# Two blocks of a transformer on one core: the modulation's weighted sum moves from GpSimd to VectorE, its loads from the sync queue to GpSimd's

## The reference

```python
mod = silu(c) @ w_mod[l] + b_mod[l]          # 2048 x 6144: shift, scale, gate
shift, scale, gate = split(mod, 3)
h = rms_norm(x, g_pre[l]) * (1 + scale) + shift
...
x = x + gate * rms_norm(y, g_post[l])
```

## Time and profile before

| | |
|---|---|
| Median of 3 runs | 4131.22 us (4123.99 to 4135.74) |
| Span of the profiled execution, first to last instruction | 4126.4 us |
| Its own time | the page gives no other than the span; the median of the runs is 4.8 us above it |
| TensorE busy | 3789.4 us (92%) |
| VectorE busy | 1773.6 us (43%) |
| ScalarE busy | 1140.1 us (28%) |
| GpSimd busy | 977.8 us (24%) |
| Moved by DMA | 430.07 MB, mean 104 GB/s |

### The profile page before, as it was taken

One profiled execution on the slowest core, in us unless ns is written; L12 is line 12 of the kernel. 1 busy time (PEld: TensorE's weight loads), 2 busy tenths in 40 slices (PEclk: granted clock), 3 DMA queues, 4 the chain that ended last, 5 costly groups with the idle time before them and its releaser, 6 DMA issues.

```text
span 4126.4 us, 54228 instructions
## 1 busy us (share of the span) xinstructions
PE 3789.4 (92%) x17149; PEld 2959.1 (72%) x17149; DVE 1773.6 (43%) x2992; ACT 1140.1 (28%) x1952; POOL 977.8 (24%) x842
## 2 busy tenths in 40 slices
PE   7999898899799988889979999997897999998898
PEld 5777677578677766756868876785686887786586
DVE  3342762542534266253352335346525224534643
ACT  3232151132313114213232224223223223422231
POOL 6746726200475673530000000003000000000300
PEclk9999899999899999999989985898899997599799
DMA  6645415133464552422233320220333321032042
GB/s 228 188 128 161 143 53 175 53 113 105 146 190 124 164 158 64 151 77 92 94 111 93 102 62 1 85 91 1 143 93 112 96 88 41 8 101 66 1 163 102
DMA packets 211419, 430.07 MB, mean 104 GB/s; under 512 B 21206, under 2 KB 28785, under 8 KB 204824
## 3 DMA queue, kind: packets, MB, share of 16 engines
q1 hardware_dynamic: 206952, 402.96, 31.2%
q10 hardware_dynamic: 2928, 21.02, 1.2%
q0 software_dynamic: 1344, 3.76, 0.4%
HBM read 406.58 MB, written 24.75 MB: 105 GB/s over the span
## 4 chain that ended last, share of the span: by engine, by line
PE 75%; POOL 9%; DVE 7%; issue 5%; DMA 2%; ACT 1%; POOLq 0%; DVEq 0%; SPq 0%; ACTq 0%
PE bank L642 17%; PE bank L644 17%; PE bank L643 17%; PE bank L677 7%; PE bank L695 5%; POOL macc L1865 5%; POOL mprod L1858 4%; PE bank L686 3%; PE bank L669 2%; DMA stage<-in_w_in 1%; PE bank L665 1%; PE bank L656 1%; DVE late L1720 1%; PE bank L796 1%; DMA wmod<-in_w_mod 1%
## 5 line engine op out<-in xcount | busy, mean ns | idle before, releaser
L642 PE MATMUL bank<-wlo,act_hi 128*128 128x512 f32 (+1 forms) x3968 | 1571.3, 396 | 100.5 <-DVE wlo L1189 52.0
L643 PE MATMUL bank<-whi,act_hi 128*128 128x512 f32 (+1 forms) x3968 | 1551.7, 391 | 0.0
L644 PE MATMUL bank<-whi,act_lo 128*128 128x512 f32 (+1 forms) x3968 | 1550.0, 391 | 0.0
L1189 DVE TENSOR_TENSOR wlo<-stage,whi 128x1024 fp32r<-128x1024 f32 (+1 forms) x496 | 645.1, 1308 | 1338.7 <-ACT whi L943 1335.3
L943 ACT ACTIVATE whi<-stage 128x1024 fp32r<-128x1024 f32 (+1 forms) x496 | 516.1, 1048 | 1628.1 <-DMA stage<-in_w_in 865.4
L642 PEld LDWEIGHTS bank<-wlo,act_hi 128*128 128x128 f32 x3968 | 755.7, 190 | 285.2 <-DVE wlo L1189 64.7
L644 PEld LDWEIGHTS bank<-whi,act_lo 128*128 128x128 f32 x3968 | 755.6, 190 | 156.4
L643 PEld LDWEIGHTS bank<-whi,act_hi 128*128 128x128 f32 x3968 | 756.9, 191 | 148.3
L1858 POOL TENSOR_SCALAR mprod<-wmod,csil 128x512 f32<-128x512 f32 x384 | 366.8, 955 | 806.7 <-DVE Y L1349 309.0
L1900 POOL TENSOR_TENSOR late<-late 128x512 f32<-128x512 f32 x48 | 66.8, 1403 | 2026.3 <-DVE late L1737 2026.3
L1865 POOL TENSOR_TENSOR macc<-macc,mprod 128x512 f32<-128x512 f32 x360 | 512.4, 1423 | 66.0 <-POOL mprod L1858 66.0
(11 more groups left out here) (198 smaller groups left out, 2516.3 us busy)
## 6 DMA issues: line engine op xcount, KB each, us to landing
stage<-in_w_in SPq DMA_DIRECT2D x352, 512.0 KB, 3.8
wmod<-in_w_mod SPq DMA_DIRECT2D x384, 256.0 KB, 2.9
stage<-in_w_out SPq DMA_DIRECT2D x128, 512.0 KB, 3.7
out<-Y ACTq DMA_DIRECT2D x20, 1024.0 KB, 5.0
zone<-out SPq DMA_DIRECT2D x4, 4096.0 KB, 14.6
stage<-in_w_in SPq DMA_DIRECT2D x16, 320.0 KB, 3.3
Y<-in_x SPq DMA_DIRECT2D x4, 1024.0 KB, 9.1
rpb_tiles<-rpb_pad POOLq DMA_DIRECT2D x16, 224.0 KB, 4.4
```

Source lines behind the costliest of these rows:

```text
L642: pe.matmul(out, hi_x, lo_w, start=(k == 0), stop=False)
L643: pe.matmul(out, hi_x, hi_w, start=False, stop=False)
L644: mm = pe.matmul(out, lo_x, hi_w, start=False, stop=(k == KC - 1))
L1189: dve.tensor_tensor(wlo[:, j % RH, :, 0:width], stage[:, j % RS, :, 0:width], whi[:, j % RH, :, 0:width].bitcast(F32), ALU.subtract).then_ ...
```

## The change

- VectorE takes the sum: a new `mod_pair` does two tiles, each in one instruction macc = wmod * column + macc (the first of a panel is a plain product). A pair follows each of the eight splits of a panel. Before the first tile it waits until TensorE has summed the macc of the panel before.
- The twelve modulation panels no longer lie in the twelve w_in panels. They go with panels 0 to 6, 9 and 10 and with output panels 13, 14 and 15, so that the panels with extra work on VectorE (7, 8, 11) have none.
- GpSimd computes nothing of it. It issues the loads of w_mod (`mod_loads`), each as soon as its buffer is free, from its own queue. It builds the bias tiles first.
- The sync queue loads w_in without modulation loads in between.
- TensorE's row sum comes one panel later, after the first double of that panel, and ScalarE sends the row out in that panel. The last one stands after panel 15.
- The squares of the output panels go to a new buffer junk in place of macc.

```diff
@@ sync @@
-            def mod_double(l, p, j):
-                for k in (2 * j, 2 * j + 1):
-                    sp.wait_ge(mod_used.sem, mod_used.at(0, l, p * KC + k + 1 - 2))
-                    ...
             def in_panel(l, p, col, width=PW):
                 for j in range(ND):
                     double(0, l, p, j, io["w_in"], col, width)
-                    mod_double(l, p, j)
@@ tensor @@
                     if j < ND - 1:
                         mm.then_inc(w_used.sem, 1)
+                    if j == 0 and row is not None:
+                        mod_row_sum(l, row)
...
-                in_panel(l, 0, src=xs)
+                panel(0, l, 0, src=xs)
                 with pe.Fori(1, 4) as p:
-                    in_panel(l, p)
+                    panel(0, l, p, row=p - 1)
...
-                with pe.Fori(4, 9) as p:
-                    in_panel(l, p)
+                with pe.Fori(4, 8) as p:
+                    panel(0, l, p, row=p - 1)
+                panel(0, l, 8)
...
-                in_panel(l, 9)
-                in_panel(l, 10, B_CKV_W)
-                in_panel(l, 11)
+                panel(0, l, 9)
+                panel(0, l, 10, B_CKV_W, row=7)
+                panel(0, l, 11, row=8)
...
-                with pe.Fori(NIN + 1, NP) as p:
-                    panel(0, l, p)
+                panel(0, l, NIN + 1)
+                with pe.Fori(NIN + 2, NP) as p:
+                    panel(0, l, p, row=p - 5)
+                mod_row_sum(l, NIN - 1)
@@ vector @@
+            def mod_pair(l, q, i):
+                for k in (2 * i, 2 * i + 1):
+                    m = q * KC + k
+                    dve.wait_ge(mod_landed[k % 2].sem, ...)
+                    if k == 0:
+                        dve.wait_ge(mod_sum.sem, mod_sum.at(0, l, q))
+                        dve.tensor_scalar(macc[:, :], wmod[:, 0, :], csil[:, 0:1], None, ALU.mult)\
+                           .then_inc(mod_used.sem, 1)
+                    else:
+                        dve.wait_ge(mod_used.sem, mod_used.at(0, l, m))
+                        dve.scalar_tensor_tensor(out=macc[:, :], in0=wmod[:, k % 2, :], scalar=csil[:, k:k + 1],
+                                                 in1=macc[:, :], op0=ALU.mult, op1=ALU.add).then_inc(mod_used.sem, 1)
...
+                    if mod is not None:
+                        mod_pair(l, mod, j - LEAD)
+                for j in range(LEAD):
+                    if after:
                         split_lo(blk, l, p + 1, j, next_width)
+                    if mod is not None:
+                        mod_pair(l, mod, ND - LEAD + j)
@@ gpsimd @@
-            def mod_panel(l, p):
+            def mod_loads(l, p):
                 for k in range(KC):
-                    ...
-                    pool.tensor_scalar(mprod[:, :], wmod[:, k % 2, :], csil[:, k:k + 1], 0.0, ALU.mult, ALU.add)
-                    ...
-                        pool.tensor_tensor(macc[:, :], macc[:, :], mprod[:, :], ALU.add)
+                    pool.wait_ge(mod_used.sem, mod_used.at(0, l, p * KC + k + 1 - 2))
+                    src = io["w_mod_2"][bass.ds(l, 1), k * P:(k + 1) * P, bass.ds(p * PW, PW)]
+                    pool.dma_start(wmod[:, k % 2, :], src.rearrange("o p n -> (o p) n"))\
+                        .then_inc(mod_landed[k % 2].sem, 16)
             for l in range(2):
-                mod_panel(l, 0)
                 ...
                 bias_tiles(l)
-                with pool.Fori(1, NIN) as p:
-                    mod_panel(l, p)
+                with pool.Fori(0, NIN) as p:
+                    mod_loads(l, p)
```

More of the change, by code:

```diff
@@ L621, in _, with panel @@
         def _(pe):
-            def panel(blk, l, p, width=PW, src=None, n0=0):
+            def panel(blk, l, p, width=PW, src=None, n0=0, row=None):
                 if src is not None:
@@ L944, in split_hi, with panel @@
                    .then_inc(hi_done.sem, 1)
-            def panel(blk, l, p, take, width=PW, after=True, next_width=PW, between=None, turned=None):
+            def panel(blk, l, p, take, width=PW, after=True, next_width=PW, between=None, turned=None, row=None):
                 if turned:
@@ L959, in panel @@
                         split_hi(blk, l, p + 1, j, next_width)
+                if row is not None:
+                    mod_row_out(l, row)
                 if take:
@@ L1049, in attention, with out_panel @@
                         exp(blk, l, br, i)
-            def out_panel(blk, l, p, after, turned=None):
-                panel(blk, l, p, None, after=after, turned=turned)
+            def out_panel(blk, l, p, after, turned=None, row=None):
+                panel(blk, l, p, None, after=after, turned=turned, row=row)
                 for t in range(TT):
@@ L1190, in split_lo, with panel @@
                                   whi[:, j % RH, :, 0:width].bitcast(F32), ALU.subtract).then_inc(lo_done.sem, 1)
[L1192 removed]
+            def mod_pair(l, q, i):
+                for k in (2 * i, 2 * i + 1):
+                    m = q * KC + k
+                    dve.wait_ge(mod_landed[k % 2].sem, mod_landed[k % 2].at(0, l, 16 * (q * (KC // 2) + i + 1)))
+                    if k == 0:
+                        dve.wait_ge(mod_sum.sem, mod_sum.at(0, l, q))
+                        apart(dve)
+                        dve.tensor_scalar(macc[:, :], wmod[:, 0, :], csil[:, 0:1], None, ALU.mult)\
+                           .then_inc(mod_used.sem, 1)
+                    else:
+                        dve.wait_ge(mod_used.sem, mod_used.at(0, l, m))
+                        apart(dve)
+                        dve.scalar_tensor_tensor(out=macc[:, :], in0=wmod[:, k % 2, :], scalar=csil[:, k:k + 1],
+                                                 in1=macc[:, :], op0=ALU.mult, op1=ALU.add).then_inc(mod_used.sem, 1)
+            def panel(blk, l, p, take, width=PW, after=True, next_width=PW, between=None, turned=None, mod=None):
                 if turned:
@@ L1202, in panel @@
                         between(j)
-                if after:
-                    for j in range(LEAD):
+                    if mod is not None:
+                        mod_pair(l, mod, j - LEAD)
+                for j in range(LEAD):
+                    if after:
                         split_lo(blk, l, p + 1, j, next_width)
+                    if mod is not None:
+                        mod_pair(l, mod, ND - LEAD + j)
                 if take:
@@ L1334, in attention, with out_panel @@
                         finish(blk, l, br, i - 3)
-            def out_panel(blk, l, p, after, between=None, turned=None):
-                panel(blk, l, p, None, after=after, between=between, turned=turned)
+            def out_panel(blk, l, p, after, between=None, turned=None, mod=None):
+                panel(blk, l, p, None, after=after, between=between, turned=turned, mod=mod)
                 for t in range(TT):
```

84 lines of the change are left out of this document (30 added, 54 removed).

## The result

The changed kernel takes 4060.55 us (median of 4 runs, 4055.24 to 4063.91), the kernel before 4133.48 in the same rounds (4123.99 to 4136.10): a ratio of 0.9821, 95% interval 0.9805 to 0.9838. It is faster by 73 us, and the profiled spans differ by 4126.4 - 4059.6 = 66.8. The forecast was 4018, a gain of 113.5. The time lies 43 us above it: inside the wide range of 4002 to 4080, which was drawn so as to take in rivals 1 (in part), 2 and 3, and outside the 4004 to 4040 that the prediction gave to its own account at a chance of 0.58. In a later round of experiments the kernel before took 4118 to 4141 us in eleven executions and 4063 and 4067 in two others, at a mean granted clock of 0.937 against 0.917 to 0.925, so that small differences between kernels of different rounds are read from windows and not from medians.

The account below looks back on a forecast made before the run. GpSimd's modulation work was taken as pacing TensorE, by holding w_in loads and stretching VectorE in block 1. Panels 113.5 us, plus 2 for row sums, minus 2 at the start, gave 4012.9, as median 4018; range 4002 to 4080.

Parts of the forecast that it names:

- rival 1: GpSimd's loads land late, VectorE holds TensorE in some ten panels per layer; gain gone at a 5.9 us cycle, chance 0.09.
- Rival 2: VectorE's two-input work holds GpSimd's load issues; cycle 5.5 us at full effect, costing 56 us, about 4074; chance 0.04.
- Rival 3: Panels 7 and 8 stay VectorE-bound, each RoPE keeping about 10 us; 30 us lost, so 4048; chance 0.12.
- GpSimd's compute and the stretching go away: Block 1: GpSimd's two instructions per tile vanish; panel 7 falls to 45.1 us, panel 8 to 46.0, RoPE to about 7.
- VectorE has room: Plain panels: 0.84 us a tile, 13.4 per panel, takes VectorE to 24 to 31 of 43.6 us, hidden if not kept waiting.
- one cycle is then 4.55 ... the limit is 5.1: Modulation panels: one buffer's round takes 4.55 us per pair of tiles; panels grow only above 5.1 us per cycle.
- Panel 2: Block 1: forecast at 44.6 us, its 5.9 us of mask work fitting partly into a load wait and 3.8 us left.
- Panels 10 and 11: Block 1: the cycle binds in 320-wide panel 10, 38.8 us instead of 45.6; panel 11 takes 46.8.
- The start: GpSimd's early bias-tile traffic delays the loading of x by 3 us, 1 comes back in the normalisation; cost 2 us.
- The moved row sums: Sums leave the ends of panels 0, 3, 8 and 11, three others are paid; about 1 us gained per layer.
- the clock after a pause: Panel 11: a lower granted clock after a pause adds 2.2 us to 44.6, giving 46.8.
- The stronger rule that the prediction weighed: GpSimd's load issues: VectorE's two-port fast modes lock GpSimd out of writing descriptors; only a panel's first tile could hold one.

Follow-up runs that it names:

- filler run: Changed kernel plus GpSimd's former product and addition on private data, 32 pairs per layer from panel 7 on; median 4095.77 us (3962.17 to 4099.53), only its trace read.
- four buffers: Changed kernel with four wmod buffers instead of two, also called the four-buffer kernel; 3996.76 us, ratio 0.968.
- split kernel: Changed kernel, two buffers, with the bias tiles loaded in four pieces and w_uq and w_ukv in six; 4035.87 us, ratio 0.9783.
- two-sum kernel: Changed kernel, two wmod buffers, with two macc accumulators in turn, so the first tile waits for the row sum one panel earlier; 4029.12 us, ratio 0.9755.
- kernel with sync loads: Changed kernel, two buffers, with w_mod loads back on the sync queue and layer 2's bias tiles built late in layer 1; 4016.39 us, ratio 0.9783.
- late-bias kernel: Four-buffer kernel with GpSimd's first-layer bias tiles built only after the first two w_in doubles are split; 3985.54 us, ratio 0.9715.

## Why the prediction was right in sign and too high in gain

- *GpSimd's compute and the stretching go away:* right. Panels 7 and 8 were forecast at 45.1 and 46.0 and are 44.7 and 44.7. Rival 3 did not come; the uncontended RoPE of about 7 us is 7.1. That GpSimd and VectorE hold each other up, as the Trainium skill has it for two-input instructions (SBUF — State Buffer, "SBUF: two separate sides"), the filler run confirms with 1.23 against 2.17.
- *VectorE has room:* right. Its tile took 0.75 instead of 0.69. With four buffers a panel with modulation takes 44.7, the forecast's 44.6, and VectorE needs 2.7 us for a wlo and a pair where TensorE takes 5.44.
- *The step that failed is "one cycle is then 4.55 ... the limit is 5.1", used as one number for all eight cycles of a panel.* The undisturbed cycle is 4.75 to 4.8: release to issue 0.71 instead of 0.3, landing 3.1 to 3.2 instead of 3.4, work 0.75 instead of 0.69. That alone would be harmless. But the last pair took 3.6 instead of 1.7, so that the chain ends at 43.5 and not at 39.8 of a panel, and the bulk loads were left out. The bias tiles and w_uq/w_ukv already went out in panels 1 and 9 before the change, and tile loads beside them were as late: the chain of the kernel before has one, issued by the sync queue at 124.27, 1.8 us behind the bias tiles (start, us, what):

```profile
124.27 9.07 DMA wmod<-in_w_mod
```

  One in panel 9 took 8.7. The earlier trace rows show a longest landing of 20.3, but the forecast took the median of 2.9. It asked how long a mean round is, and not whether a chain with one such load in it still ends before the copies are due. It is rival 1 in a local form: not a cycle that is too long everywhere, but late pairs in two panels of twelve, and a panel 10 that is too short for the cycle of two buffers at all. That the time fell into the wide range is owed to the room left for this and other rivals, not to the forecast's own sum. Panel 2: 44.6 forecast, 51.8 and 53.3 measured, 15.9 us in both layers. That the bulk load is the cause is shown by the split kernel (45.2); that lack of slack turned it into a stall is shown by the two-sum kernel (45.5) and by four buffers (44.7).
- *Panels 10 and 11:* 38.8 forecast, 39.5 measured; 46.8 forecast for panel 11, 54.4 and 54.1 measured, 14.9 in both layers. The 39.5 agree with 38.8 by chance. The forecast ended panel 10's chain after 38.1 us and put the whole wait into that panel; the chain ended at 674.6, 46.9 after the panel's start. Against the kernel with four buffers panel 10 lost 10.2 and panel 11 another 9.6. Panels 10 and 11 together are 93.9 in layer 0, where the forecast had 85.6. The sum of panel 9, itself held up by w_uq and w_ukv, ended only at 629.7, the first tile of panel 10 came at 634.8, 7.1 into the panel, and the cycles are 4.7 to 5.8. TensorE stalls 6.3 for the copies in panel 11, at a clock of 0.88. An earlier first tile and smaller loads took 3 to 4 us off panel 10 and nothing off panel 11 (54.4 and 54.0); the kernel with sync loads shows that an undisturbed cycle, and a faster one, is still too long (31.6 and 51.8), and four buffers mend both (29.3 and 44.8). The forecast named the clock after a pause as 2.2, but had the pause in panel 10.
- *The rest of the panels,* with 0.5 to 1.6 each above the forecast in panels 1, 3, 5 and 10, up to 0.3 in 4 and 6, and 3.4 in all below it in 7 and 8, adds 4.6. So the panels gave 78.1 of the 113.5 that were forecast for them.
- *The start:* 2 forecast through a late x, 3.4 measured through something else. x let ScalarE start at 18.55 (18.67 before); the first w_in double was split at 27.91 (25.30 before). The late-bias kernel shows that the cause is GpSimd's early traffic, since there TensorE starts at 33.3 although x comes later (19.87); the bias tiles and the tile loads behind them were not tried apart.
- *The moved row sums:* forecast about 1 us gained per layer. The output panels 12 to 15 with the end of the layer give 0.6 back in layer 0 (3.1 longer, the next gap 3.7 shorter) and take 6.4 in layer 1, where TensorE waits 2.04 us for VectorE's Y (L1353) before panel 15 and then shows a clock of 0.96. The chain of panel 14 ends 46.3 us after the panel's start there, and after 44.5 in layer 0. With four buffers panels 14 are 44.7 and 44.8 and the stretch takes 210.0 in layer 1 instead of 214.0 (207.6 before), so 4.0 of the 6.4 are again the load cycle of two buffers, which the forecast left out of the output panels.
- *What is not of the change:* attention B of layer 0 took 117.8 instead of 110.8. The windows of the two attentions B of the four-buffer kernel show the same two lengths under the same code:

```profile
691.90:812.50 120.60, 109.30 (x416) 59.11 (x417) 44.17 (x95) 22.95 (x54) 0.00 (x0) 0.89 0.01 5
1675.50:1786.50 111.00, 99.69 (x418) 55.80 (x417) 44.26 (x97) 23.05 (x54) 0.00 (x0) 0.97 0.02 5
```

  The length goes with the granted clock, 0.89 or 0.97, and this draw was 7 us worse in the changed kernel's profile than in that of before. Against it block 2, which the change does not touch, is 5.0 us shorter in this profile (1992.4 against 1997.4). Why these stretches differ between executions is open.
- *Rival 2* did not come. GpSimd's 384 issues took 536 to 603 ns each, median 538, with wlo subtractions running beside some of them. The stronger rule that the prediction weighed was not what cost; what the queue adds to each round is 0.47 us from release to issue, and 0.1 (median) to 0.3 (best) at the landing. The Trainium skill (DMA: Bandwidth & Descriptors, "Latency and other measured facts") gives the first byte of a GpSimd-issued transfer as about 1 us against 0.6. The traces time the whole landing and not the first byte: the same tile landed after 3.2 from GpSimd and after 3.1 from the sync queue at the median, and after 2.9 and 2.6 at best.

## What to carry to other kernels

When an in-order engine takes over a consumer that had its own slack, work out the slack of its chain to the end of the stage, last item included, and then lay every bulk transfer of the stage beside it: a mean cycle that fits says nothing of the one load that meets 2 MB, and here such a load stood in the trace of before. Two more small buffers were worth 64 us here by the medians (4060.6 to 3996.8), more than splitting the bulk loads (25) or starting the chain earlier (31), and with them splitting gained nothing; the earlier start was not tried beside them. A stage that is shorter than its neighbours, as the panel of 320 columns, is where a cycle that fits elsewhere does not, and the stall shows one stage later.

## What the runs showed of the hardware

- A tile load of 256 KB issued by GpSimd with an address from loop registers went out 0.71 us after its release and occupied GpSimd for 0.54; by the sync engine 0.24 and 0.33. The landings were 3.2 and 3.1 at the median, 2.9 and 2.6 at best.
- A 256 KB load that starts beside a 1.8 MB load into SBUF landed after 8.0 instead of 3.1 us, and one beside 2.6 MB after 7.8. The next one behind the 1.8 MB, issued 2.2 us later, still took 7.7. It did not matter which engine issued the small load: from the sync queue it took 9.1 before the change and 8.0 in the kernel with sync loads.
- GpSimd, on a buffer that VectorE does not touch, and VectorE stretched each other: 12.3 against 7.1 us for a RoPE, 1.24 against 0.70 (median) for GpSimd's product, and in one panel that made 19 us.
- A VectorE instruction of two SBUF inputs, a scalar and 128x512 float32 took 0.75 us, a subtraction of that size 0.69, a product with a scalar alone 0.49.
